# Two attentions stepped through by pairs of heads, with their values by block of queries

## What is computed

```python
# first block: adaptive modulation, token mixer, convolutional feed-forward
q, k, v, glu_a, glu_b, gate_a, gate_b = split(h @ w_in + b_in)
a  = chunked_rel_attention(q, k, v, rel_bias) @ w_attn_o     # 8 heads of 64; a query sees its own
                                                              # 64-token chunk and all before it, plus a relative bias
cb = silu(layer_norm(causal_dwconv(glu_a * sigmoid(glu_b), 31 taps))) @ w_conv_o + b_conv_o
y  = (sigmoid(gate_a) * a + sigmoid(gate_b) * cb) @ w_mix_o
# second block, layer 1: windowed attention, 16 query heads of 64, 4 key/value heads
logits = q @ k.T * scale - slope * dist                      # |distance| <= 128
probs  = softmax(concat([logits, sink]))[..., :-1]
y  = ((probs @ v) * silu(z)) @ w_out
# second block, layer 2: latent attention, 16 heads of 64 + 32, all keys (not touched by the change)
```

## Time and profile before

| what | us |
|---|---|
| median of 3 runs | 1631.37 (1629.52 to 1631.49) |
| the profiled execution | 1629.4 |
| its span, first to last instruction | 1627.6, mean granted clock 0.960 |
| first attention, first to last score | 198.3 to 342.9 |
| second attention, first to last score | 971.2 to 1107.0 |

### The profile page before, as it was taken

How to read it: one execution, slowest core, us unless ns; L and a number is a source line. 1 busy time by engine, 2 the same in 40 slices (tenths; PEclk the granted TensorE clock), 3 DMA queues, 4 the chain that set the end, 5 groups by cost and what they waited for, 6 DMA issues and landing times.

```text
span 1627.6 us, 19607 instructions
## 1 busy us (share of the span) xinstructions
PE 1500.0 (92%) x6834; PEld 1171.8 (72%) x6834; DVE 976.9 (60%) x1541; ACT 738.3 (45%) x1265; POOL 239.0 (15%) x215
## 2 busy tenths in 40 slices
PE   5898799989978999999998999998999989999897
PEld 3686576768746888887884877777777768777775
DVE  5669876556665555553225447775563558787454
ACT  4424455663334455453215226664442446666342
POOL 3006623231100000000000000111110012222111
PEclk8999899989998999999999999999999999999998
DMA  9522133335511332323221221112222120000221
GB/s 386 197 90 91 52 110 124 108 122 175 200 52 53 102 97 83 103 90 103 91 91 55 91 78 64 46 51 91 78 84 84 53 90 14 27 27 27 104 78 65
DMA packets 39881, 151.65 MB, mean 93 GB/s; under 512 B 4784, under 2 KB 4928, under 8 KB 39040
## 3 DMA queue, kind: packets, MB, share of 16 engines
q1 hardware_dynamic: 29664, 105.92, 19.9%
q0 software_dynamic: 10144, 44.76, 7.5%
HBM read 144.37 MB, written 6.29 MB: 93 GB/s over the span
## 4 chain that ended last, share of the span: by engine, by line
PE 76%; DVE 12%; ACT 5%; issue 4%; DMA 1%; POOL 0%; DVEq 0%; ACTq 0%; SPq 0%; POOLq 0%
PE ps L596 24%; PE ps L598 22%; PE ps L597 22%; PE ps L699 3%; DVE w_lo L1416 2%; PE ps L653 2%; ACT w_hi L984 2%; DMA w_raw<-in_w 1%; PE ps L673 1%; DVE c_acc L1493 1%; DVE tmp L1621 1%; ACT pt_hi L1062 1%; DVE pt_lo L1546 1%; DVE a_lo L1626 1%; DVE acc_b L1464 0%
## 5 line engine op out<-in xcount | busy, mean ns | idle before, releaser
L596 PE MATMUL ps<-a_hi,w_hi 128*128 128x512 f32 x880 | 362.1, 411 | 20.1 <-ACTq L1240 11.8
L597 PE MATMUL ps<-a_lo,w_hi 128*128 128x512 f32 x880 | 350.2, 398 | 0.0
L598 PE MATMUL ps<-a_hi,w_lo 128*128 128x512 f32 x880 | 350.1, 398 | 0.0
L1416 DVE TENSOR_TENSOR w_lo<-w_raw,w_hi 128x1024 fp32r<-128x1024 f32 x130 | 167.4, 1289 | 166.4 <-ACT w_hi L984 165.7
L596 PEld LDWEIGHTS ps<-a_hi,w_hi 128*128 128x128 f32 x880 | 167.1, 190 | 67.4 <-ACTq L1240 12.7
L598 PEld LDWEIGHTS ps<-a_hi,w_lo 128*128 128x128 f32 x880 | 166.8, 190 | 40.2
L597 PEld LDWEIGHTS ps<-a_lo,w_hi 128*128 128x128 f32 x880 | 167.5, 190 | 34.8 <-issue 0.5
L984 ACT ACTIVATE w_hi<-w_raw 128x1024 fp32r<-128x1024 f32 x138 | 144.5, 1048 | 72.9 <-PE ps L598 56.8
L1062 ACT ACTIVATE pt_hi<-ps 128x512 fp32r<-128x512 f32 (+3 forms) x160 | 79.5, 498 | 115.7 <-PE ps L699 114.9
L1546 DVE TENSOR_TENSOR pt_lo<-ps,pt_hi 128x512 fp32r<-128x512 f32 (+3 forms) x160 | 90.3, 565 | 41.1 <-ACT pt_hi L1062 38.4
L596 PE MATMUL ps<-b_hi,w_hi 128*128 128x512 f32 x240 | 99.1, 413 | 10.3 <-DVE b_lo L1784 5.6
(11 more groups left out here) (299 smaller groups left out, 2983.7 us busy)
## 6 DMA issues: line engine op xcount, KB each, us to landing
w_raw<-in_w SPq DMA_DIRECT2D x198, 512.0 KB, 3.5
ada_a<-in_ada POOLq DMA_DIRECT2D x16, 512.0 KB, 7.7
ada_g<-in_ada POOLq DMA_DIRECT2D x16, 512.0 KB, 3.8
ada_b<-in_ada POOLq DMA_DIRECT2D x16, 512.0 KB, 4.4
x_resid<-in_x POOLq DMA_DIRECT2D x2, 2048.0 KB, 11.7
pl_store<-pl_out POOLq DMA_DIRECT2D x2, 2048.0 KB, 8.8
pl<-pl_store POOLq DMA_DIRECT2D x2, 2048.0 KB, 8.8
alibi<-in_alibi POOLq DMA_DIRECT2D x16, 192.0 KB, 3.2
```

Source lines behind the costliest of these rows:

```text
L596: pe.matmul(o, w[0], r[0], start=start, stop=False, skip_group_check=skip)
L597: pe.matmul(o, w[0], r[1], start=False, stop=False, skip_group_check=skip)
L598: return pe.matmul(o, w[1], r[0], start=False, stop=stop, skip_group_check=skip)
L1416: dve.tensor_tensor(w_lo[:, n % SLOTS, :], w_raw[:, n % RAW, :], w_hi[:, n % SLOTS, :].bitcast(F32), ALU.subtract).then_inc(w_lo_done, 1)
```

## The change

Heads of the first two attentions are taken in pairs. Steps keep their count and numbers, but within a pair of heads the order is block by block: step i is head 2 pair + i % 2, block (i % 8) // 2. At each even i PE issues the scores of both heads, part by part in turn (`pair_scores`), into the two banks, and waits beforehand for the maxima of all steps before. `turn` stays one per step. The transposed blocks get a slot per step (n % 4) and lie contiguously. The values of the two steps of a pair are made at even i, for steps i - 6 and i - 5, over one block of 128 queries at a time (`pair_values`); an output bank now holds two query blocks of two heads, not four of one. It is read out in two operations of 64 partitions by 256 columns (`out1`, `out2`). The biases get four slots each: `rel` slots 2 and 3 lie at 93 KiB and in the rope table, and are loaded after the GLU; `alibi` moves to 100 KiB, `rope_k` to 106 KiB, and the rope table is loaded ahead of the second attention, with a wait of its own before the third. The third attention keeps its order in functions of its own (`attention3`, `scores3`, `values3` and so on).

```diff
@@ tables
-        rel = at("rel", 65, [P, 2, TOK])
+        rel = [at("rel0", 65, [P, TOK]), at("rel1", 67, [P, TOK]), at("rel2", 93, [P, TOK]), rope]
-        alibi = at("alibi", 88, [P, 2, 384])
+        alibi = at("alibi", 100, [P, 4, 384])
-        rope_k = at("rope_k", 70, [P, TOK])
+        rope_k = at("rope_k", 106, [P, TOK])
+            def step(self, i):
+                pair, s = divmod(i, 2 * NT)
+                return 2 * pair + s % 2, s // 2
@@ gpsimd
-            pool.dma_start(rope[:, :], t_rope).then_inc(consts_in, 16)
-            pool.memset(rel[0:CHUNK, :, TOK - CHUNK:TOK], MASKED).then_inc(rel_ready, 1)
-            load_rel(0)
-            load_rel(1)
+            for h in range(4):
+                if h == 2:
+                    pool.wait_ge(R["glu"], CT)
+                pool.memset(rel[h][0:CHUNK, TOK - CHUNK:TOK], MASKED).then_inc(rel_ready, 1)
+                load_rel(h)
-                h = (u + 1) // 2 + 1
-                if u % 2 and h < H1:
-                    pool.wait_ge(m_ready, NT * (h - 1))
-                    load_rel(h)
+                if u in (3, 7):
+                    pool.wait_ge(m_ready, 2 * NT * (u // 4 + 1))
+                    load_rel(u // 2 + 3)
+                    load_rel(u // 2 + 4)
-                    for h in range(A_HEADS):
-                        if h >= 5 and h % 2:
-                            pair_lo(o_pair2, b_hi, b_lo, (h - 5) // 2, 0, R["o2"])
-                        if h >= 2:
-                            pool.wait_ge(m_ready, attn2.n0 + NT * (h - 1))
-                        pool.dma_start(alibi[:, h % 2, :], t_alibi[h]).then_inc(alibi_in[h % 2], 16)
+                    pool.dma_start(rope[:, :], t_rope).then_inc(rope_in, 16)
+                    for pair in range(A_HEADS // 2):
+                        if pair >= 2:
+                            pool.wait_ge(m_ready, attn2.n0 + 2 * NT * (pair - 1))
+                        for h in (2 * pair, 2 * pair + 1):
+                            pool.dma_start(alibi[:, h % 4, :], t_alibi[h]).then_inc(alibi_in[h % 4], 16)
+                        if pair >= 3:
+                            pair_lo(o_pair2, b_hi, b_lo, pair - 3, 0, R["o2"])
@@ tensor
-            def scores(a, h, t):
-                n = a.n0 + NT * h + t
-                elif n >= 2:
-                    pe.wait_ge(m_ready, n - 1)
-                mm3(ps[:, S_BANK + n % 2, 0:P * (e - b)], cols(q, P * t), cols(k, P * b, P * (e - b)), True, True).then_inc(s_done, 1)
+            def pair_scores(a, i):
+                n = a.n0 + i
+                if n:
+                    pe.wait_ge(m_ready, n)
+                h, t = a.step(i)
+                b, e = a.spans[t]
+                q = [cols(a.q(h + j), P * t) for j in range(2)]
+                k = [cols(a.k(h + j), P * b, P * (e - b)) for j in range(2)]
+                for part, (w, r) in enumerate(((0, 0), (0, 1), (1, 0))):
+                    for j in range(2):
+                        m = pe.matmul(ps[:, S_BANK + j, 0:P * (e - b)], q[j][w], k[j][r], start=(part == 0), stop=(part == 2))
+                        if part == 2:
+                            m.then_inc(s_done, 1)
+            def pair_values(a, i):
+                pe.wait_ge(pt_ready, a.n0 + i + 2)
+                h, t = a.step(i)
+                b, e = a.spans[t]
+                tile = a.lin(h + t // 2)
+                if t % 2 == 0:
+                    free_bank(tile)
+                for j in range(2):
+                    at, slot = 2 * P * j + t % 2 * P, (a.n0 + i + j) % 4
+                    for s in range(b, e):
+                        m = mm3(ps[:, tile % LIN, at:at + P], a.v(h + j, s), tuple(pt[:, slot, P * s:P * s + P] for pt in a.pt),
+                                s == b, s == e - 1, skip=True)
+                m.then_inc(lin_done if t % 2 else v_half, 1)
+            def pair_attention(a, after, between=None):
+                pe.wait_ge(stat_free, events[0])
+                for i in range(a.steps + NT + 1):
+                    if i < a.steps and i % 2 == 0:
+                        pair_scores(a, i)
+                    if between is not None:
+                        between(i)
+                    if 0 <= i - 3 < a.steps:
+                        turn(a, i - 3)
+                    if i % 2 == 0 and 0 <= i - 6 < a.steps:
+                        pair_values(a, i - 6)
+                    after(i)
@@ scalar
-                act.activation(a.pt[0][:, b:e, P * t:P * t + P],
-                               ps[:, T_BANK + n % 2, P * b:P * e].rearrange("p (s q) -> p s q", q=P), ACT.Copy).then_inc(pt_hi_done, 1)
+                if t % 2 == 0 and (t or pair):
+                    act.wait_ge(v_half, a.n0 // NT + 2 * pair + t // 2)
+                elif t == 3 or pair:
+                    act.wait_ge(lin_done, a.lin(2 * pair + t // 2 - 1) + 1)
+                act.activation(a.pt[0][:, n % 4, P * b:P * e], ps[:, T_BANK + n % 2, P * b:P * e], ACT.Copy).then_inc(pt_hi_done, 1)
@@ vector, maxima
-                    if t < 2:
-                        if t == 1 or h:
+                    if t == 0:
+                        if h >= 2:
                             dve.wait_ge(e_done, n - 1)
                         dve.tensor_copy(minus_s[:, n % 2, 0:1], least)
@@ vector, outputs
-                    if t == 1 and 2 <= h < a.heads + 2:
-                        half_out(h - 2)
+                    if i % 4 == 1 and i >= 9:
+                        pair_out(i // 4 - 2)
+            def out2(j):
+                pair, q = j // 2, slice(2 * P * (j % 2), 2 * P * (j % 2) + 2 * P)
+                if j % 2 == 0:
+                    dve.wait_ge(R["z_a"], pair + 1)
+                    if pair >= 2:
+                        dve.wait_ge(R["o2"], pair - 1)
+                src = bank(attn2.lin(j))
+                for h in range(2):
+                    m = dve.tensor_tensor(o_pair2[half(h), pair % 2, q], src[half(h), 2 * P * h:2 * P * h + 2 * P],
+                                          z2[half(h), pair, q], ALU.mult)
+                m.then_inc(o_full if j % 2 else R["o2_half"], 1)
```

More of the change, by code:

```diff
@@ L792, in mixer_rest @@
                     conv_square(i - LN_SQUARE)
-            attention(attn1, after=mixer_rest, between=first_gates)
+            pair_attention(attn1, mixer_rest, first_gates)
             pe.wait_ge(pt_ready, n1)
@@ L967, in _ @@
             queries(1)
[L968 removed]
+            attention3(own_head, mla_piece)
             rest("b", A, B, R["o3"])
@@ L1065, in attention @@
-            def attention(a, outs, after=None, first=None):
-                for i in range(NT * a.heads + NT + NT):
-                    h, t = divmod(i, NT)
-                    if first is not None:
-                        first(h, t)
-                    if 0 <= i - 3 < NT * a.heads:
-                        turn_hi(a, *divmod(i - 3, NT))
-                    if h < a.heads:
-                        exps(a, h, t)
-                    if 0 <= i - 1 < NT * a.heads:
-                        norms(a, a.n0 + i - 1)
-                    if after is not None:
-                        after(h, t)
-                    if t == (3 if a is attn3 else 2) and h >= 3 and h % 2 == 1:
+                    act.wait_ge(lin_done, attn3.lin(h - 1) + 1)
@@ new lines, in turn_hi3, with pair_attention @@
+                act.activation(pt3_hi[:, :, P * t:P * t + P],
+                               ps[:, T_BANK + n % 2, :].rearrange("p (s q) -> p s q", q=P), ACT.Copy).then_inc(pt_hi_done, 1)
+            def pair_attention(a, outs, after):
+                for i in range(a.steps + 2 * NT):
+                    if 0 <= i - 3 < a.steps:
+                        pair_turn_hi(a, i - 3)
+                    if i < a.steps:
+                        exps(a, i)
+                    if 0 <= i - 1 < a.steps:
+                        norms(a, i - 1)
+                    after(i)
+                    if i % 8 == 6 and i >= 14:
+                        outs(i // 8 - 1)
@@ L1080, in attention, with attention3 @@
+            def attention3(outs, after, first):
+                for i in range(attn3.steps + 2 * NT):
+                    h, t = divmod(i, NT)
+                    first(h, t)
+                    if 0 <= i - 3 < attn3.steps:
+                        turn_hi3(*divmod(i - 3, NT))
+                    if h < B_HEADS:
+                        exps(attn3, i)
+                    after(h, t)
+                    if t == 3 and h >= 3 and h % 2 == 1:
                         outs(h // 2 - 1)
@@ L1550, in attention @@
-            def attention(a, outs, after=None, first=None):
-                half_out, pair_lo = outs
-                last = NT * a.heads
-                for i in range(last + NT + NT):
-                    h, t = divmod(i, NT)
-                    if first is not None:
-                        first(h, t)
-                    if h < a.heads:
-                        maxima(a, h, t)
-                    if 0 <= i - 1 < last and a is not attn3:
```

(22 more changed lines are left out.)

267 lines of the change are left out of this document (136 added, 131 removed).

## The result

The changed kernel takes 1636.05 us (median of 8 runs, 1634.16 to 1640.26), the kernel before 1629.18 beside it (8 runs, 1628.22 to 1631.83): ratio 1.0041, 95% interval 1.0030 to 1.0052. It is slower, by 6.9 us, or 4.7 against the median of 1631.4 that the forecast was set against; the forecast was +11.2. The profiled execution of after took 1634.16 us, 4.8 more than the one of before.

What follows compares the result with a forecast made beforehand. PE was taken to bound both attentions, the first not throughout. Second attention +6.4 and first +4.8 gave +11.2: 1642.6 us against the median of 1631.4, range 1630 to 1657.

Steps and rivals of the forecast that it cites:

- the scores' term: Paired scores in the second attention: matmuls overlap, weight loads follow 0.11 apart; saves 1.9 us per pair, bounds 1.1 to 2.9.
- the ends of the attention: Last eight steps of the second attention: sooner odd scores set against longer last values, 0, within 1.5 us either way.
- both halves fully beside each other: Rival, scores on PE: matmuls and weight loads of both row halves overlap fully; 1632 us, chance 0.24.
- the second attention's sum: Values' cost less scores' saving over eight head pairs, all on PE: +6.4 us, bounds -2.4 to +12.8.
- The values' term: Values on PE, 60 matmuls of 128 columns for 36 mixed: adds 2.6 to 2.7 us per pair.
- The rival of 81 ns a matmul: Rival, values on PE: 128-column matmuls cost less than 0.11 us in long runs; 1621 us, chance 0.05.
- The first attention's sum: Waits, value matmuls and tail of the first attention together: +4.8 us, bounds 0 and +11.
- The waiting for maxima: First attention, up to the column means: scores(16) wait for maxima(15), means come 1.5 us later, bounds 0 and +3.
- Maxima(27): Layer norm at the first attention's end: the pair of scores(28) waits for these maxima; +1.5 us, bounds 0 and +5.
- The last values: End of the first attention: they wait for the last transposed block, 24 matmuls where 12 were; +1.3 us.
- The tighter wait as a rival: Rival: PE waits in each pair, 0.3 us per second-attention pair step, 3 us more in the first; 1655 us, chance 0.11.
- What I costed at nothing: Halved output reads and sink copies, contiguous transposed blocks, POOL's waits and bias loads, later rope table: 0 us.

Runs made afterwards that it cites:

- early maxima: The changed kernel, but DVE takes an odd step's maxima right behind the even step's, in both attentions: 1635.24 us, ratio 1.0029 to the kernel before.
- the control: The changed buffers and loads with no pairs in either attention, otherwise as the kernel before: 1628.54 us, ratio 0.9996 to the kernel before.
- a ring of three half heads: Pairs in the second attention only, values over two query blocks from such a ring: 1614.95 us, ratio 0.9912; with early maxima in that attention 1609.41 us.

## Why the prediction was right and wrong

The direction held and the time lies in the range; the size did not hold, and what looks like one error of 4 to 6 us is two larger ones that partly cancel. That the time lies in the range, and even that the kernel is slower as forecast, is in part luck: the -3.8 that the second attention measured and the +4.8 that I had for the first would have made +1.0, which can't be told from no change.

- **The step that failed is the scores' term, "the matmuls overlap but weight loads follow one another at 0.11", saved 1.9 us a pair** (2.0 by its own terms, 5.84 - 3.84). It measured 3.1 (20.7 - 17.6). With the values at 2.5 for 2.7 a head pair comes to -0.6 where I had +0.8, and eight of them make 11.2 us; the ends of the attention, which I had set at 0, took 1.0 back, which leaves the 10.2 between +6.4 and -3.8. The row that I chose as nearest shows successive loads of all 128 rows; it could not say what two halves do, and I had also argued that nothing showed two loads at once, which a trace with no such pair cannot show. The rival "both halves fully beside each other" described the chip: 0.73 us for a pair of 384, loads included, its six starts within 0.46 us, where I had put 0.36 to 0.51 for full overlap. The rule of the Trainium skill that I set beside it (TensorEngine Tiling (Array Packing), Key Properties: different tiles execute weight loads and matmuls in parallel) agrees with these rows. I gave that case 0.24; with its terms the second attention's sum was -2.4 to -1.6, and it measured -3.8.
- **The values' term held.** 0.11 from start to start in runs of 128-column matmuls at the full granted clock, and 2.5 us a pair when measured alone. The start of a run costs 0.03 more than a step, not the 0.08 that I carried over from 256-column runs: 4 x 0.05 is the difference. The rival of 81 ns a matmul, the figure of the Trainium skill (TensorE: Matmul & The Clock Gate, Back-to-back issue gap), is not what this stream shows.
- **The first attention's sum, +4.8, measured +11.5**, of which 1.9 came back in the stages behind it. That stretch took 606.9 to 608.2 us in all five traces with pairs in the first attention and 609.8 to 610.1 in the six where the first attention is as before (608.8 with values by block alone), so it goes with what the change does there; what brings it back was not looked for. By stretch: to the means +4.4 (83.7 us for 79.3); means to last square sum -0.3; to the last turn, 47.6 for 43.4 us, +4.3; from there to the modulation sum +3.2.
 The waiting for maxima I placed at step 16 only, "no loss beyond it". PE waits at four pairs ahead of the means. Counted from the first score, maxima(15) itself ended 1.9 us later than in the kernel before, and the work between that pair and the means took 10.0 us, not 9.0: 1.5 + 1.9 + 1.0 = 4.4. The 9.0 was the right price at full clock (PE is busy for 9.04 us there before, at 1.00). Behind the wait the granted clock fell, and the stretch lengthened with it: 10.0 us at 0.83, 11.0 at 0.73 in two other traces, 11.5 at 0.70 in a third. Read so, a wait of PE costs more than its own length, and my sum had no term for that; no run changed the clock alone. That the waits made pair 16 late is shown by early maxima (68.4 us for 73.7). What made maxima(15) itself late, the waits before, the values by block (which alone bring the means 2.7 us later) or stretched work on DVE, is not settled.
 Maxima(27): I took 1.5 of a wait of up to 5; the wait was 5.3 and removing it in that pair gave 2.9. Of step 16 I had said that gates and turns queued behind the waiting score are not needed yet. Here they were: ACT's copy of the next turned block waited 2.60 us for PE.

```profile
341.54 0.28 ACT L1105 ACTIVATE pt_hi<-ps 128x128 fp32r<-128x128 f32 x1 [2.60 <-PE ps L727]
```

 The last values: I took "24 matmuls where they were 12", +1.3. It is 42 behind the last turns, for two heads and for both of their last query blocks, where 18 stood. My price was wrong too: most take 0.21 us each, at a granted clock of 0.57 behind idle stretches of PE, and so they did before (0.21 at 0.50), which the trace of before could have told me. +3.2, and leaving two thirds out gave it all back. In the kernel with values by block but no pairs this tail did not grow (18.5 us from the last score to the modulation sum, 18.2 before), so it comes with the pairing.
- **The tighter wait as a rival** was priced in the second attention, where it cost nothing with PE full (no wait mid-way), and costs some 5.5 us once PE is relieved (1614.95 against 1609.41). The mechanism was right and its place wrong: it decides where PE has slack, in the first attention.
- **What I costed at nothing** held for bias slots, the rope table and POOL's waits (the control, 0.9996). The outputs read in halves have no run of their own; they stand in the version with pairs in the second attention, which gained.

## What to carry to other kernels

Two matmul chains on the two 64-row halves of the array cost what one costs here (0.73 us at 384 columns); look for pairs that share a passage and keep both chains in the queue together. But price what the pairing does to its neighbours: here the layout that came with it took back 2.5 of 3.1 us per pair, and a ring of three half heads in place of four blocks avoided that. Where a wait gets tighter, look at the stretches in which the waiting engine is not full, at what the granted clock does behind a wait of PE, and at the end of the loop, where twice as much now stands behind the last step.

## What the hardware showed that I had not expected

- The halves run beside each other even when the queue holds three matmuls of one half and then three of the other: common starts, 0.73 us for the six, 1625.3 against 1624.7 us.
- DVE operations that read and write buffers of 128 partitions outside PSUM, and that started within an addition on POOL, lasted until 0.1 to 0.6 us behind its end in these places: a norm 2.16 us for 0.41, a split 2.85 for 0.69, a tap 2.79 for 0.74. Splits and maxima that read PSUM kept their time beside the same additions. Where such an operation was already running as the addition started, it was mostly the addition that grew: in the kernel before, the same split starts 0.02 us ahead of one and takes 0.68, and the addition 2.92 for 2.35. The order of DVE's work decides whether it meets one.
- The granted clock was 0.57 in the last 12 us of the first attention, behind idle stretches of PE (before 0.50 at the same place), and a tail matmul there took 0.21 us for 0.11; PE's 5.28 us of waiting at 337.32 was followed by 3.7 us at 0.50, in which a pair of 384 columns took 1.3 us.
